# A sandwich-normalised hybrid encoder step: the mean and variance products move into the middle of a block's product, and one group of loads moves in ScalarE's order

## The chip, the cores and the metric

The kernel runs on one core of a Trainium2 chip. The metric is device time in microseconds, lower is better. Before the change it is 3343.79 us, the median of three runs (3343.49 to 3347.4).

## The reference, cut to what matters

One layer of a streaming encoder, for 2048 prompt tokens and 64 sample tokens (2112 columns in all), model width 1024. A convolution branch and a sparse attention branch share one input projection; their outputs are projected, gated and added:

```python
def conv_branch(a, conv_prev, conv_w, conv_b, ln_g, ln_b):
    ...
    y = lax.conv_general_dilated(up, conv_w, ...) + conv_b
    y = jax.nn.silu(layernorm(y, ln_g, ln_b))
    return y, up[:, -(CONV_W - 1):]

def sublayer(...):
    ...
    y_c = (y_c * jax.nn.silu(g_conv)) @ w_conv_out
    y_a = (o * jax.nn.silu(g_attn)) @ w_attn_out
    gm_c, gm_a = jnp.split(jax.nn.sigmoid(gm), 2, axis=-1)
    y = (gm_c * y_c + gm_a * y_a) @ w_out
    y = rmsnorm(y, g_post)
    return x + gate[:, None] * y, conv_new, k, v, ki
```

The change concerns the stage that works out `gm_c * y_c + gm_a * y_a`, with the layernorm of the convolution's output in it.

## The kernel before

The program has five stages, each ended by all engines: front, gate (the input projection, the convolution, the key selection), attention, branch and output. Only the branch stage (`branch_stage`) and two methods of `Products` are touched.

**Tiling.** Channels lie on the 128 partitions, in KC = 8 groups; tokens are columns. The 2112 columns are two halves of W = 1056, and a half is three parts of CW = 352 columns. There are four runs, in this order: run 0 is attention, half 0; run 1 attention, half 1; run 2 convolution, half 0; run 3 convolution, half 1. A run has eight blocks, one for each group of 128 output channels. Blocks are numbered n = 8r + k (run r, place k in it); b = k % 2 picks one of two buffers.

**A block.** The 32-bit operands are split into a high and a low part, and a product is the sum of three (high by high, high by low, low by high). So one block is 8 input groups × 3 × 3 parts of columns = 72 matmuls of 352 columns, into three banks of psum[b]. `Products.product` (matmul on line 717) goes input group by input group. `Products.product_by_thirds` (line 701) finishes one part of 352 columns before the next; it is used at the last block of runs 0 and 1, where the semaphore `s_third` tells that a third of the activations has been read for the last time, and at the first block of runs 2 and 3, where each third waits for its low part. For each block:
- SyncE loads the weights (679), and stores a finished block's output (2137).
- GpSimd splits the weights, two instructions (685 and 687). The split of block n waits for the product of block n - 2.
- TensorE works the product. It waits for the split, and for the eviction of block n - 2.
- ScalarE's queue loads the block's gate (2202) and, in runs 2 and 3, the attention branch's result (2208).
- VectorE evicts: PSUM times gate into `stage` (2441), and in runs 2 and 3 adds the attention's result (2446).

**The norm.** In runs 1 and 2 the layernorm, swish and gate of the convolution's output are worked beside the products: half 0 during run 1, half 1 during run 2. The convolution's outputs y are loaded by `load_y` (2169, 2171), called on ScalarE in the last block of the run before, into the place of activations that the run has read: load j waits for the j-th third of that block, the last for the whole block. The parts of the norm are numbered q = 3·half + j. `normed(r, slot)` gives the part that is in a slot of run r, if there is one. In block k of run 1 or 2 the engines do, each in the order of its own program:
- VectorE: centre part k - 1 (2404; reads the mean from PSUM), add up part k's eight channel groups in three additions (2394, 2396, 2398), scale part k - 3 (2410 to 2419), low part of k - 5 (2432), gating product of k - 4 (2426), and then the block's eviction.
- ScalarE: the block's gate load, in the last block of runs 0 and 1 `load_y`, then squares of part k - 1 (2214), root of k - 3 (Ln and Exp, 2224 and 2226, with the load of its gate ahead, 2220), cast of k - 5 to its high part (`high`, 2232), swish of k - 3 (2239, eight instructions).
- GpSimd: the split of the block's weights, then three additions of the squares of part k - 2 (2283).
- TensorE: the block's product, and behind it `sums(k)` (2334), the mean of part k by a product with a matrix of 1/1024, and `variance(k - 2)` (2343), the same of the squares. `sums` waits for part k's third addition; both write to the fourth bank of a PSUM tensor, beside the product's three.

The order on each engine is the order of these written programs; nothing reorders them. The lines that set it in the program of TensorE are:

```python
for n, (r, k, b) in enumerate(BLOCKS):
    ...
    pr.product(pe, b, n // 2, *acts[r % 2], ready=s_flo if n == 0 else None)
    ...
    for q, part in ((normed(r, k), sums), (normed(r, k - 2), variance)):
        if q is not None:
            part(q)
```

Of the kernel before, what the change touches and what calls it, by code (L numbers as in the profile page):

```python
# [27 lines left out]
KC = D // P  # L28
# [635 lines left out]
class Products:  # L664
# [22 lines left out]
        self.nc.gpsimd.tensor_tensor(self.wlo[b][:], self.raw[b][:], self.whi[b][:].bitcast(F32),  # L687
                                     ALU.subtract).then_inc(self.s_split, 1)

    def product_by_thirds(self, pe, b, before, ahi, alo, ready=None, done=None):  # L690

        pe.wait_ge(self.s_split, 2 * before + b + 1)
        if is_later(before):
            pe.wait_ge(self.s_read, 2 * before + b - 1)
        for j in range(3):
            if ready is not None:
                s_ready, first = ready
                pe.wait_ge(s_ready, first + j + 1)
            for c in range(KC):
                for k, (w, a) in enumerate(((self.whi, ahi), (self.whi, alo), (self.wlo, ahi))):  # L700
                    last = self.nc.tensor.matmul(self.psum[b][:, j, 0:W // 3], w[b][:, c, :], a[:, c, j * (W // 3):(j + 1) * (W // 3)],
                                                 start=(c == 0 and k == 0), stop=(c == KC - 1 and k == 2))
            if done is not None and j < 2:
                last.then_inc(done, 1)
        last.then_inc(self.s_mm, 1)

    def product(self, pe, b, before, ahi, alo, ready=None):

        pe.wait_ge(self.s_split, 2 * before + b + 1)
        if is_later(before):  # L710
            pe.wait_ge(self.s_read, 2 * before + b - 1)
        for c in range(KC):
            if ready is not None:
                pe.wait_ge(ready, c + 1)
            for k, (w, a) in enumerate(((self.whi, ahi), (self.whi, alo), (self.wlo, ahi))):
                for j in range(3):
                    last = self.nc.tensor.matmul(self.psum[b][:, j, 0:W // 3], w[b][:, c, :], a[:, c, j * (W // 3):(j + 1) * (W // 3)],  # L717
                                                 start=(c == 0 and k == 0), stop=(c == KC - 1 and k == 2))
        last.then_inc(self.s_mm, 1)


# [1350 lines left out]
def branch_stage(nc, mem, x, w, out, scr):  # L2072
# [5 lines left out]
    CW, NCH = W // 3, 3  # L2078
    BLOCKS = [(r, k, k % 2) for r in range(len(runs)) for k in range(KC)]
    HALVES = 2 * KC  # L2080
    with ExitStack() as ctx:
# [73 lines left out]
        def _(act):  # L2155
# [86 lines left out]

            for n, (r, k, b) in enumerate(BLOCKS):
                load_gate(n)
                if r < 2 and k == KC - 1:
                    load_y(r)
                if n == 1:
                    for c in range(KC):
                        first_high(c)
# [1 line left out]
                for q, part in ((normed(r, k - 1), squares), (normed(r, k - 3), root), (normed(r, k - 5), high), (normed(r, k - 3), swish)):  # L2251
                    if q is not None:
                        part(q)
                if r == LAST:
                    if k == 1:
                        load_out()
# [47 lines left out]
        def _(pe):  # L2304
# [43 lines left out]
            for n, (r, k, b) in enumerate(BLOCKS):  # L2348
                if k == 0:
                    if r == 1:  # L2350
                        pe.wait_ge(s_acts, 2 * KC)
                if r >= 2 and k == 0:
                    pr.product_by_thirds(pe, b, n // 2, *acts[r % 2], ready=(s_nlo, NCH * (r - 2)))
                elif r < 2 and k == KC - 1:
                    pr.product_by_thirds(pe, b, n // 2, *acts[r % 2], done=s_third)
                else:
                    pr.product(pe, b, n // 2, *acts[r % 2], ready=s_flo if n == 0 else None)
                if n in (1, 3):
                    turn(n // 2)
                for q, part in ((normed(r, k), sums), (normed(r, k - 2), variance)):  # L2360
                    if q is not None:
                        part(q)
                if r == LAST and k in (3, 5):
                    spread(k - 3)
                    spread(k - 2)
# [288 lines left out]
```

## Time and profile before

| what | value |
|---|---|
| median of three runs | 3343.79 us |
| the profiled execution | 3353.07 us |
| its span, first to last instruction | 3351.4 us |
| TensorE busy | 3207.4 us, 96% |
| VectorE, ScalarE, GpSimd busy | 79%, 44%, 37% |
| mean granted TensorE clock | 0.983 |
| line 717's matmuls (branch stage, whole blocks) | 336.5 us, 2016 |
| line 1140's matmuls (gate stage) | 1352.1 us, 8136 |

The profile is of one execution, which took 9.3 us more than the median of the others. The branch stage's first product starts at 2731.17 us of the span and the output stage's first at 3155.81; the part with the norm, blocks 8 to 23, is 2830.41 to 3052.4. Busy time of TensorE is modelled and matmuls overlap, so its idle time and the starts of its products say more than its share.

### The profile page before, as it was taken

The numbers are of one execution on the slowest core, as the hardware profiler recorded it, in microseconds if no ns is written. First come the engines' busy times: TensorE is split into PE (matmuls) and PEld (weight loads), VectorE is DVE, ScalarE is ACT, GpSimd is POOL, SyncE is SP. The second block draws the span as 40 slices with busy tenths as digits, with TensorE's granted clock in tenths as the row PEclk, the third lists the DMA queues.
The fourth block names the chain that finished last, engine by engine and source line by source line (L and its number), as shares of the span: only waits on it lengthen the run. The fifth ranks groups of instructions, "written<-read, shape, count | busy, mean of one in ns | idle before, by whom it ended". The sixth has DMA issues, their size and how long they took to land. (4 is left out here: it accounts for less than half of the span.)

```text
span 3351.4 us, 50085 instructions
## 1 busy us (share of the span) xinstructions
PE 3207.4 (96%) x19053; PEld 2955.6 (88%) x19053; DVE 2644.9 (79%) x3935; ACT 1466.9 (44%) x1961; POOL 1251.8 (37%) x1114
## 2 busy tenths in 40 slices
PE   7999999999999999999998999999999989899998
PEld 4999888999999999999998777777777879898987
DVE  2442788998989899999996899999999965765444
ACT  2321566997950110001011677777777730432121
POOL 3322111453334400000001786777866644553200
PEclk8999999999999999999999999999999999999999
DMA  6465535445555553354445533434433355567443
GB/s 222 143 187 168 153 110 133 151 163 181 183 180 183 224 208 129 135 185 161 159 146 154 117 81 90 108 88 107 96 81 82 80 184 189 171 228 254 128 147 113
DMA packets 401941, 502.96 MB, mean 150 GB/s; under 512 B 61008, under 2 KB 316688, under 8 KB 400101
## 3 DMA queue, kind: packets, MB, share of 16 engines
q1 hardware_dynamic: 343061, 312.16, 32.1%
q10 hardware_dynamic: 51632, 158.14, 13.4%
q0 software_dynamic: 7072, 30.46, 2.3%
q8 instruction: 92, 1.51, 0.2%
q14 instruction: 84, 0.69, 0.1%
HBM read 310.63 MB, written 184.27 MB: 148 GB/s over the span
## 5 line engine op out<-in xcount | busy, mean ns | idle before, releaser
L1140 PE MATMUL psum<-ha,gt 128*128 128x352 f32 x8136 | 1352.1, 324 | 7.0 <-DVE ha L1414 4.4
L1140 PEld LDWEIGHTS psum<-ha,gt 128*128 128x128 f32 x8136 | 1322.0, 189 | 11.1 <-DVE ha L1414 4.7
L1450 DVE SCALAR_TENSOR_TENSOR cv<-cv,vecs,cv 128x1056 f32<-128x1056 f32 (+1 forms) x480 | 607.7, 1344 | 0.0
L1999 ACT CAST at<-psum 128x1024 fp32r<-128x1024 f32 (+2 forms) x308 | 289.2, 939 | 217.7 <-PE psum L1932 216.0
L1932 PE MATMUL psum<-ident,at 128*128 128x128 f32 (+1 forms) x2320 | 346.0, 272 | 17.4 <-DVE at L2064 14.6
L1932 PEld LDWEIGHTS psum<-ident,at 128*128 128x128 f32 (+1 forms) x2320 | 274.2, 141 | 98.0 <-issue 24.3
L2064 DVE TENSOR_TENSOR at<-psum,at 128x1024 fp32r<-128x1024 f32 (+2 forms) x308 | 346.0, 1126 | 7.8 <-ACT at L1999 7.3
L717 PE MATMUL psum<-br,br 128*128 128x352 f32 x2016 | 336.5, 327 | 14.0 <-DVE br L2441 9.9
L1111 POOL TENSOR_TENSOR gt<-gt,ones 128x1024 fp32r<-128x1024 f32 x60 | 123.0, 2050 | 604.5 <-PE psum L1140 604.5
L1271 ACT ACTIVATE gt<-psum 128x1056 f32<-128x1056 f32 x80 | 83.9, 1049 | 599.6 <-PE psum L1140 599.6
L717 PEld LDWEIGHTS psum<-br,br 128*128 128x128 f32 x2016 | 329.2, 190 | 18.5 <-issue 11.2
L791 DVE TENSOR_SCALAR_CACHE_REDUCE gl<-gt,gl 128x1792 bf16<-128x1792 f32 (+8 forms) x263 | 337.7, 1350 | 1.2
L1980 ACT ACTIVATE at<-at,at 128x2048 f32<-128x2048 f32 (+16 forms) x272 | 327.5, 1205 | 15.7 <-DVE at L2039 15.3
L1951 PE MATMUL psum<-at,at 128*128 128x512 f32 (+1 forms) x1160 | 328.2, 392 | 5.3 <-ACT at L2007 4.7
L762 ACT ACTIVATE gl<-gt,gl 128x2048 bf16<-128x2048 f32 (+6 forms) x224 | 314.0, 1404 | 16.3 <-DVE gl L807 12.0
L1916 PE MATMUL psum<-at,at 128*128 128x512 f32 (+5 forms) x688 | 296.4, 432 | 21.9 <-DVE at L2039 15.0
L2039 DVE CUSTOM_DVE_ANT_0 at<-psum,at,at 128x512 f32<-128x512 f32 (+5 forms) x416 | 280.9, 675 | 33.5 <-PE psum L1917 10.2
L1951 PEld LDWEIGHTS psum<-at,at 128*128 128x128 f32 x1160 | 209.8, 189 | 51.5 <-issue 8.7
L1917 PE MATMUL psum<-at,at 128*128 128x512 f32 (+5 forms) x688 | 249.4, 363 | 0.0
L1392 DVE SCALAR_TENSOR_TENSOR gt<-gt,wi,gt 128x768 f32<-128x768 f32 (+10 forms) x168 | 187.3, 1124 | 45.7 <-ACT gt L1332 38.6
L1332 ACT ACTIVATE gt<-psum 128x640 f32<-128x640 f32 (+10 forms) x192 | 153.7, 802 | 104.0 <-PE psum L1195 85.3
L1845 POOL TENSOR_TENSOR at<-at,at 128x256 f32<-128x256 f32 (+2 forms) x272 | 179.2, 660 | 35.5 <-DVE at L2039 35.4
(251 smaller groups left out, 4187.4 us busy)
## 6 DMA issues: line engine op xcount, KB each, us to landing
scratch_ws<-gt SPq DMA_DIRECT2D x112, 512.0 KB, 4.0
gt<-scratch_ws ACTq DMA_DIRECT2D x110, 512.0 KB, 4.9
gt<-in_w_in_dram SPq DMA_DIRECT2D x60, 512.0 KB, 5.7
scratch_gm<-gt ACTq DMA_DIRECT2D x32, 528.0 KB, 3.0
br<-scratch_gm ACTq DMA_DIRECT2D x32, 528.0 KB, 3.8
at<-scratch_q SPq DMA_DIRECT2D x128, 128.0 KB, 3.1
scratch_m<-br SPq DMA_DIRECT2D x30, 528.0 KB, 6.2
scratch_u<-gl POOLq DMA_DIRECT2D x16, 528.0 KB, 4.3
```

Source lines behind the costliest of these rows:

```text
L717: last = self.nc.tensor.matmul(self.psum[b][:, j, 0:W // 3], w[b][:, c, :], a[:, c, j * (W // 3):(j + 1) * (W // 3)], start=(c == 0 and k ...
L762: nc.scalar.activation(junks[(done + k) % 2][:, 0:keys_of(t)[1]], part_of(scores, t), ACT.Sign, bias=cells["candidate"][:, j:j + 1].bitcas ...
L791: nc.vector.tensor_scalar(junks[k % 2][:, 0:keys_of(t)[1]], part_of(scores, t), threshold[:, j:j + 1].bitcast(F32), None, compare, ALU.add ...
L1140: return nc.tensor.matmul(of[:, j, 0:W // 3], part[:, c, :], a[:, c, j * (W // 3):(j + 1) * (W // 3)], start=(c == 0 and k == 0), stop=(c ...
L1450: ins = nc.vector.scalar_tensor_tensor(to[:, 0:width], mine[:, k_:k_ + width], tap, to[:, 0:width], ALU.mult, ALU.add)
L1916: nc.tensor.matmul(bank(key)[:, 0:w], qhi[u % 3][:, at:at + P], kst[g % 2][:, key0:key0 + w], start=True, stop=False)
L1932: last = nc.tensor.transpose(turned[j % 2][:, k, h * n:(h + 1) * n], row_of(u)[0:n, h, b * P:(b + 1) * P], mem.ident[0:n, 0:n])
L1951: last = nc.tensor.matmul(acc[:, 0:n], vst[g % 2][:, v, :], of[:, k, 0:n], start=(part == 0 and b == 0), stop=(part == 1 and b == plan.blo ...
L1980: nc.scalar.activation(mine, mine, ACT.Exp, bias=least[0:n, u % 3, h, c:c + 1], scale=-1.0, accum_out=total[0:n, u % plan.SUMS, h:h + 1]). ...
L1999: nc.scalar.copy(phi[j % 3][:, 0:len(mine), 0:n], turned[j % 2][:, 0:len(mine), 0:n]).then_inc(s_phi, 1)
L2039: nc.vector.tensor_tensor_reduce(out=row_of(u)[0:n, h, k:k + w], in0=bank(key)[0:n, 0:w], in1=other, scale=-1.0, scalar=least[0:n, u % 3, ...
L2064: nc.vector.tensor_tensor(plo[j % 3][:, 0:len(mine), 0:n], turned[j % 2][:, 0:len(mine), 0:n], phi[j % 3][:, 0:len(mine), 0:n].bitcast(F32 ...
```

## The change

TensorE's passes for mean and variance are given to the product as a function that it calls once on its way: behind the fifth of eight input groups (`c == KC // 2`), or, where the product goes by thirds, behind the second third. In the last block of runs 0 and 1 there is no pass to give. On ScalarE, `load_y` comes behind the parts of the norm of that block instead of ahead of them.

```diff
@@ class Products
-    def product_by_thirds(self, pe, b, before, ahi, alo, ready=None, done=None):
+    def product_by_thirds(self, pe, b, before, ahi, alo, ready=None, done=None, between=None):
...
             if done is not None and j < 2:
                 last.then_inc(done, 1)
+            if between is not None and j == 1:
+                between()
         last.then_inc(self.s_mm, 1)
 
-    def product(self, pe, b, before, ahi, alo, ready=None):
+    def product(self, pe, b, before, ahi, alo, ready=None, between=None):
...
+            if between is not None and c == KC // 2:
+                between()
         last.then_inc(self.s_mm, 1)
@@ branch_stage, ScalarE
                 load_gate(n)
-                if r < 2 and k == KC - 1:
-                    load_y(r)
...
                 for q, part in ((normed(r, k - 1), squares), (normed(r, k - 3), root), (normed(r, k - 5), high), (normed(r, k - 3), swish)):
                     if q is not None:
                         part(q)
+                if r < 2 and k == KC - 1:
+                    load_y(r)
@@ branch_stage, TensorE
+                def norm_parts():
+
+                    for q, part in ((normed(r, k), sums), (normed(r, k - 2), variance)):
+                        if q is not None:
+                            part(q)
+
                 if r >= 2 and k == 0:
-                    pr.product_by_thirds(pe, b, n // 2, *acts[r % 2], ready=(s_nlo, NCH * (r - 2)))
+                    pr.product_by_thirds(pe, b, n // 2, *acts[r % 2], ready=(s_nlo, NCH * (r - 2)), between=norm_parts)
                 elif r < 2 and k == KC - 1:
                     pr.product_by_thirds(pe, b, n // 2, *acts[r % 2], done=s_third)
                 else:
-                    pr.product(pe, b, n // 2, *acts[r % 2], ready=s_flo if n == 0 else None)
+                    pr.product(pe, b, n // 2, *acts[r % 2], ready=s_flo if n == 0 else None, between=norm_parts)
                 if n in (1, 3):
                     turn(n // 2)
-                for q, part in ((normed(r, k), sums), (normed(r, k - 2), variance)):
-                    if q is not None:
-                        part(q)
```

## Rows read from the trace of the kernel before

**Rows 1.** Page of the profile, part 1: busy time, share of the span, instructions.
```profile
...
PE 3207.4 (96%) x19053; PEld 2955.6 (88%) x19053; DVE 2644.9 (79%) x3935; ACT 1466.9 (44%) x1961; POOL 1251.8 (37%) x1114
```

**Rows 2.** TensorE's timeline, branch stage: start, length (us), engine, line, count, [idle before].
```profile
...
2830.41 11.82 PE L717 MATMUL psum<-br,br 128*128 128x352 f32 x72
...
2842.39 12.04 PE L717 MATMUL psum<-br,br 128*128 128x352 f32 x72
...
2854.59 12.04 PE L717 MATMUL psum<-br,br 128*128 128x352 f32 x72
2867.65 0.86 PE L2334 MATMUL psum<-br_square,mean_ones 128*128 128x352 f32 x2 [1.02 <-DVE br_square L2398]
...
2925.06 26.14 PE L701 MATMUL psum<-br,br 128*128 128x352 f32 x144 [6.38 <-DVE br L2441]
...
2951.72 12.05 PE L717 MATMUL psum<-br,br 128*128 128x352 f32 x72
...
2963.93 12.04 PE L717 MATMUL psum<-br,br 128*128 128x352 f32 x72
2978.95 1.54 PE L2334 MATMUL psum<-br_square,mean_ones 128*128 128x352 f32 x2 [2.98 <-DVE br_square L2398]
...
3038.22 14.34 PE L717 MATMUL psum<-br,br 128*128 128x352 f32 x72 [6.39 <-DVE br L2441]
```

**Rows 3.** VectorE's timeline, branch stage, same columns.
```profile
...
2837.14 0.53 DVE L2398 TENSOR_TENSOR br_square<-br_square 128x352 f32<-128x352 f32 x1
...
2848.82 1.62 DVE L2394 TENSOR_TENSOR br_square<-br_y 128x1408 f32<-128x1408 f32 x1
2850.47 0.89 DVE L2396 TENSOR_TENSOR br_square<-br_square 128x704 f32<-128x704 f32 x1
2851.40 0.52 DVE L2398 TENSOR_TENSOR br_square<-br_square 128x352 f32<-128x352 f32 x1
...
2855.74 3.08 DVE L2404 TENSOR_TENSOR br_y<-br_y,psum 128x2816 f32<-128x2816 f32 x1
...
2864.18 3.41 DVE L2398 TENSOR_TENSOR br_square<-br_square 128x352 f32<-128x352 f32 x1
2867.52 1.24 DVE L2441 TENSOR_TENSOR br<-psum,br 128x1056 f32<-128x1056 f32 x1
...
2883.20 5.17 DVE L2419 TENSOR_TENSOR br_y<-br_y,bn 128x2816 f32<-128x2816 f32 x1
...
2923.67 1.24 DVE L2441 TENSOR_TENSOR br<-psum,br 128x1056 f32<-128x1056 f32 x1
...
2943.30 3.75 DVE L2432 TENSOR_TENSOR br<-br_y,br 128x2816 fp32r<-128x2816 f32 x1 [9.69 <-ACT br L2232]
...
2959.85 0.52 DVE L2398 TENSOR_TENSOR br_square<-br_square 128x352 f32<-128x352 f32 x1
...
2977.02 1.87 DVE L2398 TENSOR_TENSOR br_square<-br_square 128x352 f32<-128x352 f32 x1
```

**Rows 4.** GpSimd's timeline, branch stage, same columns.
```profile
...
2844.35 2.40 POOL L687 TENSOR_TENSOR br<-br,br 128x1024 fp32r<-128x1024 f32 x1
2851.58 6.24 POOL L2283 TENSOR_TENSOR br_square<-br_square 128x1408 f32<-128x1408 f32 x3 [4.83 <-ACT br_square L2214]
...
2859.74 3.65 POOL L687 TENSOR_TENSOR br<-br,br 128x1024 fp32r<-128x1024 f32 x1
```

**Rows 5.** ScalarE's timeline, branch stage, and its queue's transfers.
```profile
...
2848.93 2.56 ACT L2214 ACTIVATE br_square<-br_y 128x2816 f32<-128x2816 f32 x1 [105.90 <-DVE br_y L2404]
...
2931.94 8.05 ACTq L2169 DMA_DIRECT2D br_y<-scratch_y  x3
...
2940.71 2.56 ACT L2232 CAST br<-br_y 128x2816 fp32r<-128x2816 f32 x1 [14.39 <-issue]
```

**Rows 6.** Line 2169's loads: issue to landing.
```profile
...
DMA to landing us min/median/max: 7.5/8.0/12.4
```

**Rows 7.** Stretches (from:to, length, busy us by engine; PEclk is the granted clock).
```profile
...
2925.00:2931.00 6.00, 5.94 (x20) 5.97 (x21) 4.65 (x2) 1.32 (x1) 0.98 (x1) 0.50 0.83 265
```
## The prediction

> **What bounds the kernel now.** I read the page's shares first: TensorE is busy 96% of the span [rows 1], so a change pays or costs what it does to TensorE's idle time. Then TensorE's timeline of the branch stage: blocks 8 to 23, the second and third run, are where the norm is worked beside the products. Without the norm a block takes 11.9 us plus 0.3 for a pass of the mean or variance: block 9 starts at 2842.39, block 10 at 2854.59, 12.2 later. TensorE idles in front of the sums of the third part (1.02 and 2.98 us), and far more in front of blocks 15 and 23 (6.38 and 6.39 us), both times for an eviction by VectorE [rows 2]. That eviction is the end of a chain that goes back and forth between ScalarE (squares, root, swish, cast) and VectorE (scale, gate, low part), from the eviction of block 10, which begins at 2867.52, to that of block 13 at 2923.67 [rows 3]. So VectorE's place in its program, not TensorE's, sets the time of a half's norm. After block 23 TensorE runs without a gap to the end, and what is late there is late at the end.
>
> **Part 1, mean and variance products in mid-block.** Nothing is added or removed: 12 passes move from behind a product to behind five eighths of it (two thirds where it goes by thirds). No queue is passed; but TensorE is in order, so behind a pass that waits stand now the last 27 matmuls of the same product, and the eviction of that block behind them.
>
> What could it bring? The mean is read by the centring. In VectorE's program that stands behind the eviction of the same block, which needs the whole product: the centring at 2855.74 starts the moment the eviction is done. Variance is read by ScalarE's root, which stands behind squares that wait for a centring. So an earlier pass is worth 0, and the eviction and those squares cover it.
>
> What does it cost? The sums need VectorE's three additions of the same block, and those come after the eviction of the block before (1.2 us) and a centring (3.0). The mark in mid-block is 5/8 of 11.9 = 7.4 us after the block's start. The additions were done [rows 2, 3]:
> Block 8: 2837.67, 7.3 after its start: no stall.
> Block 9: 2851.92, 9.5 after it: a stall of 2.1.
> Block 10: 2867.59, 13.0 after it.
> Block 17: 2960.37, 8.65 after it: a stall of 1.2.
> Block 18: 2978.89, 15.0 after it.
> Alone the three take 1.62 + 0.89 + 0.52 = 3.05 us; in block 10 the last and smallest took 3.41 instead of 0.52 [rows 3], while GpSimd added squares or split weights without a pause [rows 4]. GpSimd's split, alone 2.40, took 3.65 in the same stretch [rows 4]. So they exclude each other, instruction by instruction. The Trainium skill says the same (SBUF — State Buffer, Who interferes with whom): a VectorE instruction with two SBUF inputs and a GpSimd one that reads SBUF lock each other out for a whole instruction. By that rule the centring, whose second input is PSUM, is free; the trace agrees, 3.08 beside a busy GpSimd.
>
> Block 10 walked with the new start. Block 9's stall puts it at 2856.7. Eviction and centring end at 2860.9. GpSimd is done with the first squares at 2857.8 as before, then splits until 2862.1 (1.9 + 2.4), so the first addition runs from 2862.1 to 2863.7. ScalarE's squares (2.56, [rows 5]) end at 2863.5, GpSimd asks first and gets the next turn: its three additions of squares, 6.24 together, are some 3.5, 1.8 and 0.9 by their sizes. 2867.2; second addition 2868.1; GpSimd 2869.9; third addition 2870.4. That is 13.7 after the start, and a stall of 6.3 after the mark at 2864.1. Two passes 0.65, the last 27 matmuls 4.45: the product ends, and the eviction begins, at 2875.5, against 2867.52. **+8.0 us**, carried down the chain to block 15.
>
> Second half. Block 17's stall makes block 18 1.2 late. Its additions end between 8.65 (block 17's figure, nothing in the way) and 15.0 (this block's own of before); I take 13.7, the one walked, being nearest in kind. Mark 7.4, stall 6.3, passes 0.65, matmuls 4.45: eviction 18.8 after the start, plus the 1.2, against 14.9 before. **+5.1 us**, to block 23 and the end.
>
> The clock. After the 6.38 us wait the granted clock of the next 6 us was 0.50, the lower level, 1.2 GHz [rows 7], and 144 matmuls took 26.14 instead of some 23.5: 2.6 lost. After 6.39 us, 72 took 14.34: 2.5 lost. After 1.02 us the pair of passes took 0.86 and nothing was lost; after 2.98 the pair took 1.54 [rows 2], but the slow stretch lay in product 19, beside the chain. The two new waits of 6.3 are nearest the first two, and now the slow matmuls stand ahead of the eviction: **+2.5 twice** (bounds 0 and 2.6 each).
>
> The Trainium skill describes TensorE's queue as pulling weight loads ahead of running matmuls, no matmul past another (TensorE: Matmul & The Clock Gate, the table at its top). By it the waiting pass holds the rest up, which gives my sum; if matmuls could pass, the stalls would be 0, as would the sum. The idle 1.02 us in front of a sum with block 11's matmuls behind it agrees [rows 2].
>
> **Part 2, ScalarE's loads of the convolution's outputs.** In run 0 no part of the norm exists, so the order there is the same. In block 15 one instruction changes place: the cast of the third part now comes ahead of the three load steps (four transfers of up to 1,408 KB on ScalarE's queue; the next block's gate and old loads stay behind them, and SyncE's and GpSimd's queues are not passed). The cast ran at 2940.71 behind the loads' waits. VectorE had begun to wait for it at 2943.30 − 9.69 = 2933.6, an eviction after its gate product, so the input was there at 2932.4. New: cast 2932.4 to 2935.0, VectorE's low part done by 2938 instead of 2947.0. The last third of product 16 wants it at about 2939.5 + 7.9 = 2947.4, so the gain on TensorE is 0 (bounds 0 and 0.4). The first load leaves at 2935.0 instead of 2931.94, lands 8.0 later, at the longest 12.4 [rows 6]: 2943.0 (2947.4). The additions (3.05) end at 2946.1 (2950.5), against the new mark of 2/3 of product 16 at 2947.4. Cost 0, upper bound 3.1. Had the low part stayed late, the additions would have begun at 2948.2 and the mark been missed by 3.8; part 2 is what pays that.
>
> **Sum.** 8.0 + 5.1 + 2.5 + 2.5 + 0 = +18.1 us. The profiled execution took 3353.07 us for a span of 3351.4 and would take 3371.2; it stands 9.3 above the median of the runs, 3343.79, and the same sum on the median gives **3361.9**.
>
> **Rivals.**
> A, forecast: both third additions stay entangled with GpSimd. For it: they were in both halves before, and the block's start moves by 2 us or less. 0.60.
> B, one half gets free: GpSimd's split begins on time in block 18 and is over before the centring is. Then that half costs 1.2 + 8.65 and the rest, 14.9 against 14.9, so 0, and no fall of the clock. 8.0 + 2.5 = 10.5: 3354.3. For it: the margins in the walk are 0.2 us to 1.2 us. 0.20.
> C, loads late: ScalarE's cast delays them until block 16's mark is missed: +3.1, 3365.0. Against: only the longest landing does it. 0.05.
> D, no entanglement in either half: block 10's additions end at 1.2 + 3.0 + 3.05 = 7.25, no stall there, the eviction begins 2.1 + 12.5 − 12.9 = 1.7 late; 3345.5. Or the passes do get by without holding up the product: 3343.8. 0.11.
> E, faster: the shift also frees the chain. The scaling at 2883.20 took 5.17, for a size that takes 3.08 elsewhere [rows 3], with a split in its way. If the split moves off it, in both halves, and the additions are free too, 4.2 us of the waits at blocks 15 and 23 go. Shorter waits, 4.3 instead of 6.4, may keep the clock up, 5.1 more; less D's 1.7: −7.6, 3336.2. It decides at a split that starts 2 us earlier against the scaling. Against: the split follows the product's end, which becomes later, not earlier. 0.04.
>
> **How the numbers follow.** 0.2% is 6.7 us, about what a measurement of this kernel can tell from no change. A, B and C lie above it: slower 0.85; D within it: 0.11; E: 0.04. The likeliest is A, 3361.9. Its own range by the bounds: without falls of the clock 3356.9, with block 18's additions at 15.0 and a late load 3366.3. The range of 3350 to 3367 takes in B with its margin and C, and leaves out D, E and the upper rest.
>
> **What would show it.** In TensorE's timeline products 9, 10, 17 and 18 are cut in two (45 and 27 matmuls), with idle time before the pass that names VectorE's last addition: some 2, 6, 1 and 6 us; block 8 has none. The eviction of block 10 begins some 8 us later than before, with a lower clock in the 27 matmuls ahead of it; the waits at blocks 15 and 23 stay at 6 us. The time between the evictions of blocks 10 and 13 stays near 56 us. ScalarE's cast lies ahead of the loads, and VectorE's wait of 9.69 us is gone. The prediction falls if the additions of block 10 end less than 9 us after the block's start, or if the matmuls behind a waiting pass run on.

## The result, and the profile after

| | before | after |
|---|---|---|
| median | 3344.4 us (6 runs) | 3362.81 us (6 runs) |
| ratio, 95% interval | | 1.0058 (1.0044 to 1.0073) |
| the profiled execution: span | 3351.4 us | 3361.4 us |
| branch stage: first product to the output stage's first | 424.6 us | 440.6 us |
| start of block 8 to start of block 24 | 222.0 us | 238.0 us |
| start of block 8 to end of block 24 | 233.5 us | 249.4 us |

The change makes the kernel slower by 0.58% (18.4 us between the medians). In the two profiled executions the branch stage is 16.0 us longer; the stages ahead of it happened to be 6.0 us shorter in the one of after (the first product of the branch stage starts at 2725.21 instead of 2731.17), and the output stage takes the same (195.6 us). So the stretches within the branch stage are the measure in what follows, and S is the one from the start of block 8's product to the start of block 24's. Lines of after are numbered a little higher: 719 is 717 of before, 2338 the mean, 2347 the variance, 2405 the third addition, 2448 the eviction.

TensorE's timeline of after, blocks 8 to 23 (start, length, engine, line, count, [idle before]):

```profile
...
2824.46 7.44 PE L719 MATMUL psum<-br,br 128*128 128x352 f32 x45
...
2846.23 0.86 PE L2338 MATMUL psum<-br_square,mean_ones 128*128 128x352 f32 x2 [1.98 <-DVE br_square L2405]
...
2862.24 1.54 PE L2338 MATMUL psum<-br_square,mean_ones 128*128 128x352 f32 x2 [3.52 <-DVE br_square L2405]
2863.57 1.38 PE L2347 MATMUL psum<-br_square,mean_ones 128*128 128x352 f32 x2
2864.23 12.52 PE L719 MATMUL psum<-br,br 128*128 128x352 f32 x72
...
2890.39 0.83 PE L2347 MATMUL psum<-br_square,mean_ones 128*128 128x352 f32 x2 [1.41 <-DVE br_y L2426]
...
2909.41 13.41 PE L719 MATMUL psum<-br,br 128*128 128x352 f32 x72 [2.17 <-DVE br L2448]
...
2925.99 20.89 PE L701 MATMUL psum<-br,br 128*128 128x352 f32 x120 [3.17 <-DVE br L2448]
2947.78 0.86 PE L2338 MATMUL psum<-br_square,mean_ones 128*128 128x352 f32 x2 [0.90 <-DVE br_square L2405]
...
2965.56 1.54 PE L2338 MATMUL psum<-br_square,mean_ones 128*128 128x352 f32 x2 [5.82 <-DVE br_square L2405]
...
2982.48 0.86 PE L2338 MATMUL psum<-br_square,mean_ones 128*128 128x352 f32 x2 [1.96 <-DVE br_square L2405]
...
3010.98 0.83 PE L2347 MATMUL psum<-br_square,mean_ones 128*128 128x352 f32 x2 [3.19 <-DVE br_y L2426]
...
3048.87 13.70 PE L719 MATMUL psum<-br,br 128*128 128x352 f32 x72 [6.40 <-DVE br L2448]
```

The counterpart of [rows 2]. The profile joins the end of one product with the start of the next, so the cuts are seen at the passes. Block 8's pass does not wait. Then the waits before passes: 1.98 us (block 9), 3.52 (10), 0.90 (16), 5.82 (17), 1.96 (18). Two waits of a new kind stand before a variance pass, 1.41 us in block 12 and 3.19 in block 20, both for VectorE's scaling. In front of block 15 the wait is now 3.17 instead of 6.38; in front of block 23 it is 6.40.

VectorE's timeline of after:

```profile
...
2838.90 1.26 DVE L2448 TENSOR_TENSOR br<-psum,br 128x1056 f32<-128x1056 f32 x1 [7.19 <-DMA br<-scratch_gm]
...
2851.58 1.26 DVE L2448 TENSOR_TENSOR br<-psum,br 128x1056 f32<-128x1056 f32 x1 [5.41 <-PE psum L719]
...
2857.91 0.89 DVE L2403 TENSOR_TENSOR br_square<-br_square 128x704 f32<-128x704 f32 x1
2858.83 3.35 DVE L2405 TENSOR_TENSOR br_square<-br_square 128x352 f32<-128x352 f32 x1
2869.61 1.26 DVE L2448 TENSOR_TENSOR br<-psum,br 128x1056 f32<-128x1056 f32 x1 [7.42 <-PE psum L719]
...
2921.59 3.08 DVE L2433 TENSOR_TENSOR br_y<-br_y,br_square 128x2816 f32<-128x2816 f32 x1
2924.59 1.25 DVE L2448 TENSOR_TENSOR br<-psum,br 128x1056 f32<-128x1056 f32 x1
...
2943.16 3.09 DVE L2401 TENSOR_TENSOR br_square<-br_y 128x1408 f32<-128x1408 f32 x1 [1.44 <-DMA br_y<-scratch_y]
...
2956.86 1.26 DVE L2448 TENSOR_TENSOR br<-psum,br 128x1056 f32<-128x1056 f32 x1 [9.13 <-DMA br<-scratch_gm]
```

GpSimd's of the same time:

```profile
...
2858.51 6.21 POOL L2287 TENSOR_TENSOR br_square<-br_square 128x1408 f32<-128x1408 f32 x3 [2.12 <-ACT br_square L2218]
```

Against [rows 3]: block 10's second addition went through alone (0.89), the third took 3.35. GpSimd's additions of squares had started at 2858.51, between the two. The eviction of block 10 starts at 2869.61, which on before's scale (blocks 8 laid on each other, 5.95 us to add) is 2875.56, against 2867.52: 8.0 later. The eviction of block 16, at 2956.86, waited 9.13 us for its gate. That of block 8, at 2838.90, waited for its gate too, as it did before the change (6.99 us there): both gates stand in ScalarE's queue behind a group of `load_y`.

ScalarE's queue of after at block 15, and the stretch behind block 17's wait (from:to, length, busy us of TensorE, its loads, VectorE, ScalarE, GpSimd, then the granted clock, DMA share, GB/s):

```profile
...
2934.87 2.55 ACT L2236 CAST br<-br_y 128x2816 fp32r<-128x2816 f32 x1 [7.62 <-DVE br_y L2433]
2934.88 4.96 ACTq L2173 DMA_DIRECT2D br_y<-scratch_y  x3
2939.86 3.71 ACTq L2175 DMA_DIRECT2D br_y<-scratch_y  x1
2943.61 3.28 ACTq L2206 DMA_DIRECT2D br<-scratch_gm  x1
```

```profile
...
2965.50:2971.50 6.00, 5.94 (x20) 5.45 (x21) 0.00 (x1) 0.00 (x0) 5.67 (x3) 0.54 0.22 89
```

The landing of the loads of line 2173 (2169 before):

```profile
...
DMA to landing us min/median/max: 7.4/11.6/12.6
```

The counterparts of [rows 5, 6, 7]. The cast stands ahead, the loads are issued from 2934.88 on, and the gate of block 16 is issued only at 2943.61, behind all four transfers. The loads' median landing is 11.6 us instead of 8.0. After the 5.82 us wait the granted clock was 0.54 over the next 6 us, nearly all at the lower level, as it had been before the change behind block 15's wait (0.50, [rows 7]).

### The profile page after: what moved, and what is told of

Read it like the earlier page. It is cut to its first block and busy times, and to the rows that moved or that the text cites. A ratio compares the mean times of both kernels' runs of the same rounds, so it can differ in the third digit from the quotient of the medians.

```text
span 3361.4 us, 50085 instructions
## 1 busy us (share of the span) xinstructions
PE 3206.8 (95%) x19053; PEld 2955.3 (88%) x19053; DVE 2636.4 (78%) x3935; ACT 1466.7 (44%) x1961; POOL 1248.5 (37%) x1114
## 5 line engine op out<-in xcount | busy, mean ns | idle before, releaser
L719 PEld LDWEIGHTS psum<-br,br 128*128 128x128 f32 x2016 | 333.6, 192 | 19.1 <-issue 11.6
```

## The experiments

All S are from one profiled execution each. The same part of a program varies by some 3 us between executions (below), so a difference in S under that is not read by itself, and a sum of such differences is known no better. The time's ratio to before is given where several executions of the kernel were timed; the others ran once. Half 0 below is the stretch from the start of block 8 to that of block 15, half 1 from there to the start of block 24.

| kernel | S, us | time against before |
|---|---|---|
| before | 222.0 | |
| after | 238.0 | 1.0058 |
| passes only | 236.7 | 1.0058 (1.0042 to 1.0073) |
| loads only | 220.3 | 0.9999 (0.9989 to 1.0009) |
| sums in mid-block only | 229.5 | |
| variance in mid-block only | 224.3 | |
| after, short squares | 222.6 | |
| before, short squares | 213.1 | |
| after, gate of block 16 first | 229.5 | |
| after, mark at 7/8 | 225.6 | 1.0021 (1.0008 to 1.0033) |
| before, evictions early | see there | 1.0006 (0.9995 to 1.0018) |
| before, additions first | 222.6 | 1.0006 (0.9991 to 1.0020) |
| loads only and additions first | 219.2 | 0.9994 (0.9978 to 1.0010) |

### The two parts of the change, each alone

Passes only: the change with ScalarE's loop as it was.

```diff
                 load_gate(n)
+                if r < 2 and k == KC - 1:
+                    load_y(r)
...
                         part(q)
-                if r < 2 and k == KC - 1:
-                    load_y(r)
```

> TensorE's passes in mid-block as in the change, ScalarE's loads where they were. Measure: the stretch from the start of block 8's product to the start of block 24's, 222.0 us before the change and 238.0 after it. Theory (the mid-block sums cost, and the moved loads only shift where): block 10 as in the changed kernel (idle 3.5 us before its sums); block 16's pass finds its additions late (low part done only at 2947, additions at 2951 against the mark of 2947), idle some 4 us there; its gate lands earlier than in the changed kernel, so block 17's idle time is 1 to 3 us instead of 5.8. Stretch 234 to 241, time 0.3 to 0.6% above before. Rival (most of the loss is the moved loads'): stretch under 230, less than 0.2% above before.

Measured: S 236.7, ratio 1.0058. TensorE's waits, VectorE's low part of the third part, and GpSimd's split behind it:

```profile
...
2854.50 1.22 PE L2338 MATMUL psum<-br_square,mean_ones 128*128 128x352 f32 x2 [2.03 <-DVE br_square L2405]
...
2868.83 0.86 PE L2338 MATMUL psum<-br_square,mean_ones 128*128 128x352 f32 x2 [0.28 <-DVE br_square L2405]
...
2958.08 1.54 PE L2338 MATMUL psum<-br_square,mean_ones 128*128 128x352 f32 x2 [4.09 <-DVE br_square L2405]
```

```profile
...
2926.77 4.78 DVE L2433 TENSOR_TENSOR br_y<-br_y,br_square 128x2816 f32<-128x2816 f32 x1
...
2950.05 3.79 DVE L2439 TENSOR_TENSOR br<-br_y,br 128x2816 fp32r<-128x2816 f32 x1 [8.63 <-ACT br L2236]
```

```profile
...
2928.68 5.10 POOL L687 TENSOR_TENSOR br<-br,br 128x1024 fp32r<-128x1024 f32 x1
```

The passes alone make the whole loss, in S and in time. Block 9 waits 2.03 as in after. The pass behind that wait took 1.22 instead of 0.86, and the 72 matmuls behind it 13.56 instead of 12.07 (2855.00, not in the rows): the granted clock was 0.73 over the 6 us from 2855.00, and 1.00 at that place in after. So block 10 began 1.5 us later, when GpSimd was further on, and VectorE's additions got through: block 10, with the same program as in after, waits 0.28 instead of 3.52, which the expectation had not seen. The eviction of block 10 is still 5.0 us later than before, relative to block 8 (42.1 against 37.1; 45.2 in after). In block 16 the pass waits 4.09, since the low part is done only at 2953.8 and the additions come behind it. That wait is what the loads' new place takes away (0.90 in after); block 17's wait is 1.96 here and 5.82 in after, and half 1 is as long in both (136.5 and 136.4).

Loads only: the kernel before with `load_y` behind the parts of the norm.

> The loads of the convolution's outputs behind the cast in block 15, the passes at the end of the product as before. Theory: the loads leave 3 us later, the gate of block 16 is queued behind them and lands late, and the eviction of block 16 waits for it (it began at 2951.34 before, some 4 us later in the changed kernel). Here no pass waits in mid-block, so this lateness is partly covered: the stretch of blocks 8 to 23 is 222 to 226 us against 222.0, time within 0.2%. Rival (the late gate is the whole loss of the second half): 228 or more. Second rival (the cast ahead of the loads gains): under 220.

Measured: S 220.3, ratio 0.9999. VectorE's last addition in block 16, and block 16's eviction; then TensorE's passes in blocks 17 and 18:

```profile
...
2943.41 0.52 DVE L2398 TENSOR_TENSOR br_square<-br_square 128x352 f32<-128x352 f32 x1
2952.66 1.26 DVE L2441 TENSOR_TENSOR br<-psum,br 128x1056 f32<-128x1056 f32 x1 [8.72 <-DMA br<-scratch_gm]
```

```profile
...
2961.35 0.86 PE L2334 MATMUL psum<-br_square,mean_ones 128*128 128x352 f32 x2 [1.26 <-DVE br_square L2398]
...
2977.86 1.54 PE L2334 MATMUL psum<-br_square,mean_ones 128*128 128x352 f32 x2 [3.99 <-DVE br_square L2398]
```

The late gate is there (8.72 us of wait), and most of it is covered: behind an ordinary product, block 17's sums are needed 12 us after its start and not 7. They still wait, 1.26 us in block 17 (none before) and 3.99 in block 18 (2.98 before), but the stretch is not longer for it, and the time is the same within 0.1%. As a whole the moved loads are neutral. S came out just under the 222 to 226 of the expectation, by less than it varies.

### Which pass costs

Sums in mid-block only, and variance in mid-block only, both with the loads where they were. The first is:

```diff
                 def norm_parts():
-                    for q, part in ((normed(r, k), sums), (normed(r, k - 2), variance)):
-                        if q is not None:
-                            part(q)
+                    q = normed(r, k)
+                    if q is not None:
+                        sums(q)
...
                     turn(n // 2)
+                q = normed(r, k - 2)
+                if q is not None:
+                    variance(q)
```

> Only the sums in mid-block, the variance behind the product, the loads where they were. Theory: the sums are the whole cost of the passes, so the stretch of blocks 8 to 23 is that of the kernel with both passes in mid-block within 3 us (234 to 241). Rival (the variance's waits for the centring or the scaling, 1.4 and 3.2 us idle in the changed kernel in blocks 12 and 20, cost as much): 4 us or more below it.

> Only the variance in mid-block, the sums behind the product, the loads where they were. Theory: ScalarE's root waits for its squares and not for the variance, so nothing is gained, and the variance's own inputs are nearly always there, so little is lost: stretch 221 to 225 us against 222.0. Rival (the variance pass in mid-block costs a share): 226 or more. Rival (it gains): under 220.

Measured: S 229.5 and 224.3. Over 222.0, the sums cost 7.5 us, the variance 2.4, both together 14.7. The variance alone came out in the range expected for it. The expectation that the sums are everything missed (234 to 241), and its rival held: the sums alone are 7.2 us below the kernel with both passes. One part is seen in the waits: the variance of the third part waits in mid-block for VectorE's scaling of the first (its PSUM place is the one that scaling reads), 1.41 and 3.19 us with both passes early, 0.50 and 2.92 with the variance alone, none with the sums alone.

Another part is the clock, and not the variance. Behind block 14's wait, which is 2.1 to 2.2 us in both kernels, the product ran at the full clock with both passes early (72 matmuls in 11.85 us), and at a lower one with the sums alone, 0.72 over the first 6 us. VectorE's second gating product and GpSimd's split behind product 14, with the sums alone:

```profile
...
2901.25 13.42 PE L719 MATMUL psum<-br,br 128*128 128x352 f32 x72 [2.11 <-DVE br L2451]
```

```profile
...
2913.44 3.08 DVE L2436 TENSOR_TENSOR br_y<-br_y,br_square 128x2816 f32<-128x2816 f32 x1
```

```profile
...
2914.81 3.46 POOL L685 TENSOR_TENSOR br<-br,ones 128x1024 fp32r<-128x1024 f32 x1 [10.69 <-PE psum L719]
```

The slow product ended late, the split that waits for its end started late, and the gating product came first: 3.08 us, where it took 4.78 beside the split with both passes early (the last two fences of the first experiment) and in the kernel before:

```profile
...
2918.97 4.78 DVE L2426 TENSOR_TENSOR br_y<-br_y,br_square 128x2816 f32<-128x2816 f32 x1
```

So block 15 started 16.6 us after block 14, and not 18.3. The same happened at blocks 22 and 23. That is 1.7 us in each half, 3.4 of the 7.2 us between the two kernels, which fell to the one with the sums alone by its clock. Without it the sums would have cost some 11 of the 14.7 us (an estimate from these rows).

### The memory port

By port is meant here what the prediction reads from [rows 3, 4]: an instruction of VectorE with both inputs in SBUF and one of GpSimd do not run at the same time. The change with GpSimd's additions of squares cut to 16 columns of one group (the variance is left out in all but name), and the same edit to the kernel before.

```diff
-                for i, m in enumerate((4, 2, 1)):
+                for i in range(3):
                     if i:
                         pool.wait_ge(s_sqsum, 3 * q + i)
-                    nc.gpsimd.tensor_tensor(sq[:, 0:m, at], sq[:, 0:m, at], sq[:, m:2 * m, at], ALU.add).then_inc(s_sqsum, 1)
+                    nc.gpsimd.tensor_tensor(sq[:, 0:1, at.start:at.start + 16], sq[:, 0:1, at.start:at.start + 16], sq[:, 1:2, at.start:at.start + 16], ALU.add).then_inc(s_sqsum, 1)
```

> The changed kernel, in which GpSimd's three additions of squares cover 16 columns of one group instead of all, so the variance is wrong and they hardly use the memory port. Theory (port conflict with the squares' additions stretched block 10's third addition, 3.35 us for 0.52): block 10's additions take 3.0 to 3.2 us in sum and its sums wait under 1 us instead of 3.5. The stall of 2 us in block 9 and of some 6 us in block 17 have other causes (gate loads that land late) and stay. Stretch of blocks 8 to 23: 231 to 236 us against 238.0. Rival (the port is the cause of most of the loss): under 228. Rival (no part of it): 237 or more.

> The kernel before the change with the same short additions of squares as in the changed one with short squares (the variance is wrong here too). It is that experiment's control; the stretch is taken here from the start of block 8 to the end of block 24: 233.5 us before, 249.4 changed, 234.0 changed with short squares. Theory (the change costs through waits for late additions, and the squares' hold on the port is the larger part of their lateness): without the squares the kernel before gains too, but less, since its additions were nearly covered: 226 to 231 us, so that the change costs 3 to 8 us here instead of 16. Rival (the port alone makes the loss, the place of the passes none): within 1.5 us of 234.0. Rival (the port matters as much before): 218 to 221.

Measured: after 238.0 to 222.6, before 222.0 to 213.1 (to the end of block 24: 249.4 to 234.0, and 233.5 to 224.5). The third addition of block 10 in after with short squares:

```profile
...
2854.19 0.53 DVE L2405 TENSOR_TENSOR br_square<-br_square 128x352 f32<-128x352 f32 x1
```

0.53 instead of 3.35, and the pass waits 0.28. The squares cost the changed kernel 15 us and the one before 9. They do it through the port: in blocks 8 to 23 of after, the profile shows no wait of TensorE, VectorE or ScalarE for GpSimd, so its shorter work helps by no longer stretching VectorE's. Without the squares the change still costs 9.5 us, with waits of 1.44 us in block 9 and of 1.96 in blocks 17 and 18, where nothing stretches the additions. So of the 16 us some 6.5 come from the port and some 9.5 from the place of the passes alone, each worked out from executions that vary by some 3 us. Both expectations missed their ranges: the first (231 to 236) had what the squares cost too small, the second had the gain of the kernel before too small (226 to 231, measured 224.5) and the change's rest too (3 to 8).

### The late gate of block 16

The change with block 16's gate and attention result loaded ahead of the outputs.

```diff
             for n, (r, k, b) in enumerate(BLOCKS):
-                load_gate(n)
+                if n != 2 * KC:
+                    load_gate(n)
...
                 if r < 2 and k == KC - 1:
+                    if r == 1:
+                        load_gate(n + 1)
                     load_y(r)
```

> The changed kernel, with block 16's gate and attention result loaded ahead of the convolution's outputs instead of behind them. Theory (the eviction of block 16 waited 9.1 us for its gate, which was queued behind 4.3 MB of outputs, and so made block 17's pass 5.8 us late): the eviction of block 16 starts within 1 us of the end of its product, block 17's pass waits 1 to 2.5 us, block 16's own waits up to 3 us more since the outputs land later; stretch 233 to 237 us against 238.0. Rival (the late gate is cover for a wait that comes anyhow): block 17's stall goes and block 18's grows to 5 us or more, stretch 237 or more.

Measured: S 229.5. VectorE's first addition and the eviction in block 16, and TensorE's passes in blocks 16 and 17:

```profile
...
2941.61 1.62 DVE L2404 TENSOR_TENSOR br_square<-br_y 128x1408 f32<-128x1408 f32 x1 [3.70 <-DMA br_y<-scratch_y]
...
2949.59 1.26 DVE L2451 TENSOR_TENSOR br<-psum,br 128x1056 f32<-128x1056 f32 x1 [4.87 <-PE psum L701]
```

```profile
...
2944.78 0.86 PE L2341 MATMUL psum<-br_square,mean_ones 128*128 128x352 f32 x2 [0.63 <-DVE br_square L2408]
...
2958.68 0.86 PE L2341 MATMUL psum<-br_square,mean_ones 128*128 128x352 f32 x2 [1.95 <-DVE br_square L2408]
```

The eviction now follows its product, and block 17's pass waits 1.95 instead of 5.82. The outputs are later by that (3.70 us of wait for them), which costs nothing, since block 16's pass waits 0.63 only. Half 0, the same program as in after, went as in the kernel with the passes only (13.50 for the 72 matmuls behind block 9's wait): block 10 waits 0.26, its eviction starts 42.0 after block 8 and not 45.2. So of the 8.5 us between the two kernels not all is the gate's: 1.4 arose in half 0, and of the 7.1 in half 1 1.7 are the slow product ahead of block 23, as in the experiment before (13.37 us for product 22). The gate is worth about 5, an estimate. S fell further than the expectation's 233 to 237, by these parts.

### A later mark

```diff
-            if between is not None and c == KC // 2:
+            if between is not None and c == KC - 2:
```

> The changed kernel with the passes behind the seventh of eight input groups instead of the fifth (9 matmuls of the product left instead of 27). Theory (what costs is that a pass waits for additions which end 8 to 11 us after a block's start, with the mark at 7.4): the mark is at 10.4, so the stalls of blocks 9 and 17 shrink to under 1 and some 3 us and the stretch is 224 to 231 us, time 0 to 0.3% above before. Rival (any pass inside a product costs, by the break in the product): 235 or more, 0.5% above before.

Measured: S 225.6, ratio 1.0021. The waits before sums in blocks 10, 17 and 18:

```profile
...
2866.86 0.86 PE L2338 MATMUL psum<-br_square,mean_ones 128*128 128x352 f32 x2 [2.24 <-DVE br_square L2405]
...
2964.03 0.86 PE L2338 MATMUL psum<-br_square,mean_ones 128*128 128x352 f32 x2 [1.52 <-DVE br_square L2405]
...
2982.29 1.54 PE L2338 MATMUL psum<-br_square,mean_ones 128*128 128x352 f32 x2 [5.77 <-DVE br_square L2405]
```

Block 9's wait is gone, block 17's is 1.52 with the gate still late, and three quarters of the loss in S, two thirds of that in time, are gone with 18 matmuls more ahead of the pass, as the theory had it. A break in the product as such costs nothing that shows (72 matmuls across block 8's pass took 12.07 us, an uncut product 12.04); the wait in it does. Block 18's wait of 5.77 is larger than at 5/8: here the additions met GpSimd's split and its squares, and took 3.71, 3.72 and 1.87 us for 1.62, 0.89 and 0.52.

### What would beat both

Evictions early: the kernel before, with the eviction ahead of the low part and the gating product.

```diff
-                for q, part in ((normed(r, k - 1), centre), (normed(r, k), add_up), (normed(r, k - 3), scale), (normed(r, k - 5), low),
-                                (normed(r, k - 4), gated)):
+                for q, part in ((normed(r, k - 1), centre), (normed(r, k), add_up), (normed(r, k - 3), scale)):
+                    if q is not None:
+                        part(q)
+                evict(n)
+                for q, part in ((normed(r, k - 5), low), (normed(r, k - 4), gated)):
                     if q is not None:
                         part(q)
...
-                evict(n)
```

> The kernel before, with VectorE's eviction ahead of the low part and the gating product of the same block instead of behind them. Theory (the two waits of 6.4 us at blocks 15 and 23 are VectorE's place in its program, two whole passes of 3 us each ahead of an eviction whose product has long ended): both waits and the waits at blocks 14 and 22 shrink to under 2 us, no fall of the clock there; the last third of block 16 then waits up to 3 us for its low part. Stretch 205 to 214 us against 222.0, time 0.2 to 0.5% below before. Rival (the chain behind it only moves the wait to the low parts of blocks 16 and 24): 219 or more, within 0.2%.

Measured: ratio 1.0006. TensorE at blocks 15 and 16, and VectorE:

```profile
...
2923.21 15.67 PE L701 MATMUL psum<-br,br 128*128 128x352 f32 x96 [0.59 <-DVE br L2441]
2940.08 4.13 PE L701 MATMUL psum<-br,br 128*128 128x352 f32 x24 [1.20 <-DVE br L2432]
2950.97 5.39 PE L701 MATMUL psum<-br,br 128*128 128x352 f32 x24 [6.75 <-DVE br L2432]
```

```profile
...
2927.53 5.30 DVE L2426 TENSOR_TENSOR br_y<-br_y,br_square 128x2816 f32<-128x2816 f32 x1
...
2939.95 5.26 DVE L2426 TENSOR_TENSOR br_y<-br_y,br_square 128x2816 f32<-128x2816 f32 x1
```

The wait of 6.4 in front of block 15 became 0.59. But block 16, in thirds, now waits 1.20 and 6.75 us for its low parts, and block 24 1.37 and 6.81. S, which ends with block 23, is 212.2, as the theory had it, but it misleads: block 24 ends after 234.8 us, against 233.5 before, and the time did not fall. So the rival's mechanism and its time held, though it had put S at 219 or more. In this order what bounds a half is the norm's own chain up to the last low part. The gating products there, 3.08 alone, took 5.30 and 5.26 beside GpSimd's splits.

Additions first: the kernel before with the three additions ahead of the centring, and the same with the moved loads.

```diff
-                for q, part in ((normed(r, k - 1), centre), (normed(r, k), add_up), (normed(r, k - 3), scale), (normed(r, k - 5), low),
+                for q, part in ((normed(r, k), add_up), (normed(r, k - 1), centre), (normed(r, k - 3), scale), (normed(r, k - 5), low),
```

> The kernel before, with VectorE's three additions of part k ahead of the centring of part k - 1. The passes stay behind the product. Theory (the two sums that TensorE waits for, 1.0 and 3.0 us, wait for additions stretched by GpSimd's squares, which in this order start only after the centring): both waits go, and the fall of the clock in block 18 with the second; the eviction of block 10 then starts at the end of its product. Stretch to the end of block 24: 228 to 232 us against 233.5, time 0 to 0.2% below before. Rival (GpSimd's split of the weights now stands in the additions' way, and a later centring starts the chain later): 233 to 237.

> The same, with the moved loads of the change as well, the passes behind the product: the candidate to beat both kernels. The loads alone made the stretch 231.7 us against 233.5, at an equal time. Theory: the two add, 226 to 230 us, time 0.1 to 0.3% below before. Rival: no more than either alone, 230 to 234, within 0.1%.

Measured: S 222.6 and 219.2, to the end of block 24 234.1 and 230.7, ratios 1.0006 and 0.9994. Both came out in the ranges of their rivals. VectorE's first addition in block 10, and the third addition and the centring in block 18, in the first of the two:

```profile
...
2846.34 4.36 DVE L2394 TENSOR_TENSOR br_square<-br_y 128x1408 f32<-128x1408 f32 x1
...
2964.72 2.10 DVE L2398 TENSOR_TENSOR br_square<-br_square 128x352 f32<-128x352 f32 x1
2966.75 3.08 DVE L2404 TENSOR_TENSOR br_y<-br_y,psum 128x2816 f32<-128x2816 f32 x1
```

Block 10's wait is gone. In block 18 the additions ended earlier, but the sums then wait 3.51 us for the centring behind them, which reads the mean's place. The expectation had GpSimd's squares start only after the centring, but those of the part before were on their way (from 2845.99, 7.83 us for the three), and they hold block 10's first addition instead (4.36 for 1.62). Neither version is faster than before by more than the measurement can tell. No kernel that beats both was found.

## Why the prediction was right, point by point

The forecast, 3361.9 us, lies 0.9 us from the median, and the sign and the mechanism were right. The total was nearer than its parts.

**What the passes bring.** 0, as said. None of the kernels with passes in mid-block has a shorter S than before, and the variance alone in mid-block gave 224.3 against 222.0.

**Block 9.** A stall of 2.1 was forecast; 1.98 and 2.03 were measured. The forecast took the 9.5 us from the rows without asking why they were not 7.3. They begin with block 8's eviction, which waits for a late gate in both kernels, by some 2 us. So block 9's wait is very likely a late gate's, as block 17's turned out to be; no run had that gate early.

**Block 10.** A stall of 6.3 was forecast; 3.52 was measured in after, and 0.28, 0.26 and 0.27 in the kernels with the passes only, with block 16's gate first and with the sums only. The step that failed is the turn at the memory port. The walk had GpSimd's squares ask 0.2 us ahead of the second addition, and so the third addition end 13.7 us after the block's start. In after the second addition was issued 0.6 us ahead of the squares, since block 9's eviction, and the centring and squares behind it, came 0.8 later than walked; only the third addition waited. In the other kernels hardly any did, and there the additions ended some 7.8 us after the block's start. That is less than the 9 us which the forecast had named as a sign of being wrong, and yet the kernel with the passes only is as slow (1.0058): its eviction of block 10 is still 5.0 us late, with 1.5 us of it from the lower clock behind block 9's wait. With a margin of 0.2 us the walk should have taken the freer case as likely. The mechanism is right: the cut in the squares took the 3.35 away.

In after the stall was 2.8 us shorter than walked, and the eviction of block 10 came 8.0 us late all the same, which was the forecast without its 2.5 for the clock. Three things made it up: the product reached its mark 0.6 later; the two pairs of passes behind the 3.52 us wait ran slowly (1.54 and 1.38 instead of 0.86 and 0.76) and took 1.3 more than walked; and the eviction began 5.4 us behind them and not 4.45. Of that last term half is no clock: behind block 9's pass, at the full clock, it is 4.9 (2846.66 to 2851.58). That the 8.0 was met is luck.

**Down the chain.** It was to be carried on unchanged to block 15. The eviction of block 13 is 6.9 late in after: the chain was 55.0 us instead of 56.2. The wait in front of block 15 halved, by a lower clock: product 14 took 13.4 us instead of 11.9, GpSimd's split behind it came later, and VectorE's second gating product, ahead of block 13's eviction, took 3.08 instead of the 4.78 beside the split. In the kernel with the passes only, product 14 ran at the full clock and the wait was 6.43.

**Second half.** The forecast was 1.2 in block 17 and 6.3 in block 18, with the loads at 0. It was 5.82 and 1.96. The step that failed is "the next block's gate and old loads stay behind them", which was read as no change. They do stay behind, but the last load to be issued went out at 2939.86 with the others still under way. The gate of block 16 was issued at 2943.61, and the eviction that waits for it began 4.4 us after its product's end. So VectorE was late for block 17's additions while TensorE was on time for their pass. With the gate ahead of the loads the wait was 1.95. The forecast's rival C had the loads late for block 16's own additions; that was 0.90 only. Block 18 was the free case of rival B.

**The clock.** Two falls of 2.5 us were forecast. After the 5.82 us wait there was one (0.54 granted; the next 72 matmuls took 14.14 instead of 12.07), after 3.52 a partial one. Against that, block 15's fall was smaller with its shorter wait, and the fall in product 14 gave 1.7 back. So the clock's net share was less than 5.

**The sum.** 18.1 forecast; 16.0 in the branch stage of the profiled execution, 18.4 between the medians. The terms of half 0 were too large by 3.6 us, since block 13's eviction was 6.9 late and not 10.5. The terms of half 1 were too small by 1.5: 9.1 measured against 7.6. That these errors have opposite signs, and that the medians lie 2.4 us further apart than the branch stages of the two profiles, is why the forecast missed by only 0.9; that closeness is luck, the sign and the order of size are not.

**What the forecast said would show it.** The cut products and named waits, block 8 with none, the 56 us chain (55.0), the cast ahead of the loads and the end of VectorE's 9.69 us wait were there, and block 23 waits 6.40. The 6 us wait at block 15 was not.

## What to carry to other kernels

On an in-order engine, moving a small dependent step forward into a long one helps only if the reader of its result waits for it. Here the reader stood behind the same block's end anyway, and all that was moved forward was the wait. Before such a move, list when the inputs were ready relative to the new place, block by block, from the trace. If they are later than the place in most blocks, the difference is the cost, and what follows in the same engine's queue pays it. And when a group of large loads moves in a queue, count as well when the small loads behind it land: the gate of one block, 528 KB behind 4.2 MB, cost about 5 us here (an estimate).

## What the runs showed that was not expected

A wait of 2 us by TensorE did not always leave the clock alone. Behind block 9's wait (1.98 in after; 2.03, 1.96 and 1.86 us in three kernels with the same program up to there) the next 72 matmuls took 12.07 in after and 13.56, 13.50 and 13.62 us in the others. And the fall paid for itself: it moved block 10 by 1.5 us, past GpSimd's turn at the port, and its wait went from 3.52 to 0.3 us, its eviction from 45.2 to 42.1, 42.0 and 41.3 us after block 8's start. So a change of 1.5 us ahead of a contested port came out as a change of 3 us behind it, of the other sign. The slow products 14 and 22 are the second case: in the twelve kernels that leave VectorE's eviction in its place, blocks 15 and 23 start 18.3 to 18.8 us after blocks 14 and 22, but 16.6 in the six places where the product ahead ran slow. That the slow product caused the earlier start is read from these profiles and was not tried by itself. For a learner it means that a difference of 3 us between two single profiles of this kernel says little until the clock in both has been looked at.
